# Turning the probabilities one step later, and four key sub-blocks moved between the layers

## The reference

```python
q_a = to_heads(rms_norm(c_q, q_gain) @ w_uq, MLA_HEADS)          # heads 0..3
o_a = causal_block_attention(q_a, k_a, kv_a[..., MLA_NOPE_DIM:])  # softmax(q k^T) v
o_b = causal_block_attention(q_b, k_b, v_b, cum_log_f)           # heads 4..9
o_c = dilated_mixture_attention(rope(q_c), rope(k_c), v_c)       # heads 10..15
x = layer_norm(DEEPNORM_ALPHA * x + mix @ w_out)
...
k, v = split(mem @ w_kv, 2)      # depends on mem and the layer's weights, not on x
x = layer_norm(DEEPNORM_ALPHA * x + softmax(q k^T / 16) v @ w_o)
gates = shared_group_router(x, router_w, router_bias)
x = layer_norm(DEEPNORM_ALPHA * x + moe_ffn(x, gates, w_gate, w_up, w_down))
```

## Time and profile before

| | |
|---|---|
| median of 3 runs | 820.36 us (818.98 to 822.27) |
| profiled execution: its own time | 822.08 us |
| profiled execution: span of the trace | 820.5 us |
| TensorE busy | 797.2 us, 97% of the span |
| VectorE busy | 634.1 us, 77% |
| ScalarE busy | 508.5 us, 62% |
| mean granted TensorE clock | 0.99 |

### The profile page before, as it was taken

One profiled execution on the slowest core, in us unless ns is written; L12 is line 12 of the kernel. 1 busy time (PEld: TensorE's weight loads), 2 busy tenths in 40 slices (PEclk: granted clock), 3 DMA queues, 4 the chain that ended last, 5 costly groups with the idle time before them and its releaser, 6 DMA issues.

```text
span 820.5 us, 12140 instructions
## 1 busy us (share of the span) xinstructions
PE 797.2 (97%) x4364; PEld 688.0 (84%) x4364; DVE 634.1 (77%) x1110; ACT 508.5 (62%) x804; POOL 78.4 (10%) x150
## 2 busy tenths in 40 slices
PE   7899999999999999999999999999999999999995
PEld 7899897789877888888899989877998788888884
DVE  5657868785658999999765586786846699999995
ACT  4755554554546788888555555554454567888873
POOL 3148200020000000000011350000200000000000
PEclk9999999999999999999999999999999999999998
DMA  8954443475334799999755644336643439999951
GB/s 289 344 182 155 144 135 130 139 228 157 105 126 134 246 368 367 364 370 374 259 150 146 209 142 154 105 129 204 209 129 99 145 120 342 367 369 364 370 209 52
DMA packets 122095, 177.06 MB, mean 216 GB/s; under 512 B 10177, under 2 KB 90577, under 8 KB 122033
## 3 DMA queue, kind: packets, MB, share of 16 engines
q1 hardware_dynamic: 120048, 169.56, 62.0%
q0 software_dynamic: 1984, 6.70, 2.9%
HBM read 175.18 MB, written 1.05 MB: 215 GB/s over the span
## 4 chain that ended last, share of the span: by engine, by line
PE 81%; DVE 10%; ACT 4%; issue 2%; DMA 2%; SPq 0%; POOL 0%; DVEq 0%; ACTq 0%; POOLq 0%
PE bank L1557 22%; PE bank L1559 22%; PE bank L1558 22%; DVE w_split L509 3%; DMA raw<-in_w_in_dram 2%; PE bank L1660 2%; PE bank L1724 2%; PE bank L1765 2%; PE bank L1870 2%; DVE xg_lo L1496 1%; ACT w_split L504 1%; PE bank L1756 1%; PE bank L1735 1%; PE bank L1713 1%; PE bank L1785 1%
## 5 line engine op out<-in xcount | busy, mean ns | idle before, releaser
L509 DVE TENSOR_TENSOR w_split<-raw,w_split 128x1024 fp32r<-128x1024 f32 (+3 forms) x336 | 386.0, 1173 | 69.8 <-ACT w_split L504 63.6
L504 ACT ACTIVATE w_split<-raw 128x1024 fp32r<-128x1024 f32 (+3 forms) x336 | 335.4, 1010 | 103.7 <-PE bank L1559 86.2
L1557 PE MATMUL bank<-w_split,xg_hi 128*128 128x512 f32 x256 | 102.9, 402 | 0.0
L1559 PE MATMUL bank<-w_split,xg_lo 128*128 128x512 f32 x256 | 100.1, 391 | 0.0
L1558 PE MATMUL bank<-w_split,xg_hi 128*128 128x512 f32 x256 | 99.9, 390 | 0.0
L1557 PE MATMUL bank<-w_split,xT_hi 128*128 128x384 f32 (+2 forms) x224 | 77.9, 348 | 3.1 <-DVE w_split L509 2.3
L1559 PE MATMUL bank<-w_split,xT_lo 128*128 128x384 f32 (+2 forms) x224 | 76.5, 341 | 0.0
L1558 PE MATMUL bank<-w_split,xT_hi 128*128 128x384 f32 (+2 forms) x224 | 76.2, 340 | 0.0
L1559 PEld LDWEIGHTS bank<-w_split,xg_lo 128*128 128x128 f32 x256 | 48.0, 188 | 10.3
L1557 PEld LDWEIGHTS bank<-w_split,xg_hi 128*128 128x128 f32 x256 | 48.1, 188 | 9.5 <-DVE xg_lo L1496 0.6
L1558 PEld LDWEIGHTS bank<-w_split,xg_hi 128*128 128x128 f32 x256 | 48.2, 188 | 9.0
(11 more groups left out here) (314 smaller groups left out, 1550.9 us busy)
## 6 DMA issues: line engine op xcount, KB each, us to landing
raw<-in_expert_w_gate_dram SPq DMA_DIRECT2D x128, 256.0 KB, 5.8
raw<-in_expert_w_up_dram SPq DMA_DIRECT2D x128, 256.0 KB, 7.8
raw<-in_expert_w_down_dram SPq DMA_DIRECT2D x64, 512.0 KB, 7.8
raw<-in_xattn_w_kv_dram SPq DMA_DIRECT2D x32, 512.0 KB, 4.1
raw<-in_w_in_dram SPq DMA_DIRECT2D x40, 384.0 KB, 4.0
raw<-in_w_mix_out_dram SPq DMA_DIRECT2D x16, 512.0 KB, 3.8
raw<-in_xattn_w_q_dram SPq DMA_DIRECT2D x16, 512.0 KB, 3.4
raw<-in_xattn_w_o_dram SPq DMA_DIRECT2D x16, 512.0 KB, 5.5
```

What stands on the lines that cost most here:

```text
L504: nc.scalar.activation(w_hi[:, i % SPL, 0:w], raw[:, i % RAW, 0:w], ACT.Copy).then_inc(hi_ready, 1)
L509: nc.vector.tensor_tensor(w_lo[:, i % SPL, 0:w], raw[:, i % RAW, 0:w], w_hi[:, i % SPL, 0:w].bitcast(F32), ALU.subtract).then_inc(lo_ready, 1)
L1557: nc.tensor.matmul(o, lhs[0], rhs[0], start=first, stop=False, skip_group_check=shared)
L1559: return nc.tensor.matmul(o, lhs[1], rhs[0], start=False, stop=last, skip_group_check=shared)
```

## The change

It has three parts. First, `TURNED` and `VALUED`: the probabilities are turned in step s for head s-3 in place of s-2, the values are made for head s-4 in place of s-3, and there are 20 steps. On VectorE the normalisation in step s is that of head s-2, and it and the copy of the turned head stand ahead of the maximum of head s-1. `p_sb` and `pT` become one tile with three buffers of probabilities and two of turned ones for the 16 heads. The exponentials of the dilated heads no longer give sums, which were not used. Second, in layer 1 the job MK1 is replaced by ME1 (the same weights, the same product): its four sub-blocks stand at the head of layer 1's stream, in the places where TensorE made the unread products, in pair 3; they are copied out before the head steps. Layer 0 keeps MK1, and layer 1's filler has 25 sub-blocks. A's parts 0 and 1 are then split after the transposes of x. UKV goes from pair 3 to pair 1. Third, in layer 1 the jobs from MV0 on exchange pairs 0 and 1. The lines that only pass `l` to `banks`, `evac_a` and `evac_v` are left out below.

```diff
+TURNED, VALUED = 3, 4
...
+        if l:
+            subs += [(l, "ME1", j) for j in range(4)]
         for name, js in (("A", range(4)), ("FV", range(4)), ("FK", range(4)), ("FQ", range(2)), ("UQ", range(1)),
                          ("UKV", range(1)), ("FQ", range(2, 4)), ("DQ", range(4)), ("DK", range(4)), ("DV", range(4)),
-                         ("MK0", range(4)), ("MK1", range(4)), ("MV0", range(4)), ("WO0", range(3)), ("WO1", range(1)), ("WO0", range(3, 4)), ("WO1", range(1, 4)),
+                         ("MK0", range(4)), ("MK1", range(0 if l else 4)), ("MV0", range(4)), ("WO0", range(3)), ("WO1", range(1)), ("WO0", range(3, 4)), ("WO1", range(1, 4)),
...
-        p_sb, _ = sb("p_sb", [P, 2, 4 * P])
-        pT, _ = sb("pT", [P, 2, 4 * P])
+        probs, _ = sb("probs", [P, 16 * P])
...
-                ("UQ", 2, 0, 2), ("UKV", 0, 4, 3), ("FQ", 2, 0, 0), ("DQ", 2, 0, 1), ("DK", 2, 0, 0), ("DV", 0, 2, 1),
+                ("UQ", 2, 0, 2), ("UKV", 0, 4, 1), ("ME1", 2, 0, 3), ("FQ", 2, 0, 0), ("DQ", 2, 0, 1), ("DK", 2, 0, 0), ("DV", 0, 2, 1),
...
+        def left_out(l):
+            return "MK1" if l else "ME1"
+
+        def pair_in(l, name, k):
+            return 1 - k if l and k < 2 and job[name] >= job["MV0"] else k
+
+        pair = [{name: pair_in(l, name, k) for name, _, _, k in jobs} for l in range(L)]
+
+        def held_by(l, name):
+            return next((m for m, _, _, _ in reversed(jobs[:job[name]]) if m != left_out(l) and pair[l][m] == pair[l][name]), None)
...
-        slots = [3, 2, 2] + [2, 1] * 4 + [1, 2] * 2 + [1] * 4
+        slots = [[3, 2, 2] + [2, 1] * 4 + [1, 2] + [1] * 7] + [[3, 2, 2, 2] + [1] * 16] * (L - 1)
...
+            assert len(turns[l]) == HEADS + VALUED
...
+        def probs_of(h):
+
+            if h < HEADS:
+                return probs[:, (h % 3) * 3 * P:(h % 3 + 1) * 3 * P]
+            return probs[:, (h % 2) * 4 * P:(h % 2 + 1) * 4 * P]
+
+        def turned_of(h):
+
+            if h < HEADS:
+                return probs[:, (9 + h % 2 * 3) * P:(12 + h % 2 * 3) * P]
+            return probs[:, (8 + h % 2 * 4) * P:(12 + h % 2 * 4) * P]
+
+        def free_turns(h):
+
+            return h - 2 if h < HEADS else max(h - 1, HEADS)
...
-                if h >= 2:
-                    act.wait_ge(pt_done.sem, pt_done.at(l, h - 1))
+                if h >= 3:
+                    act.wait_ge(pt_done.sem, pt_done.at(l, free_turns(h)))
...
-                        src, scale = p_sb[:, h % 2, sl], 1.0
+                        src, scale = probs_of(h)[:, sl], 1.0
...
-                    acc = sm1 if MLA_H + FOX_H <= h < HEADS else sm
-                    nc.scalar.activation(p_sb[:, h % 2, sl], src, ACT.Exp, bias=nmx[:, h, t:t + 1], scale=scale,
-                                         accum_out=acc[:, h, t:t + 1]).then_inc(e_ready.sem, 1)
+                    total = {} if MLA_H + FOX_H <= h < HEADS else {"accum_out": sm[:, h, t:t + 1]}
+                    nc.scalar.activation(probs_of(h)[:, sl], src, ACT.Exp, bias=nmx[:, h, t:t + 1], scale=scale, **total)\
+                        .then_inc(e_ready.sem, 1)
...
+            def keys(l, name, c0):
+                wait_job(l, name)
+                for u, b in enumerate(banks(l, name)):
+                    nc.scalar.activation(kTx[:, c0 + 2 * u:c0 + 2 * u + 2, :], b[:, :].rearrange("p (c t) -> p c t", c=2),
+                                         ACT.Copy).then_inc(job_a.sem, 1)
...
-                if l == 0:
-                    split_hi(act, first)
+                split_hi(act, first)
...
-                    split_hi(act, first + 1)
+                split_hi(act, first + 1)
...
+                if l:
+                    act.wait_ge(split_free, free_at(index[l, "UKV", 0]))
+                    keys(l, "ME1", 4)
...
-                for s in range(HEADS + 3):
+                for s in range(HEADS + VALUED):
...
-                    for nm, r in (("MK0", 0), ("MK1", 1)):
-                        if index[l, nm, 3] in turns[l][s]:
-                            wait_job(l, nm)
-                            for u, b in enumerate(banks(nm)):
-                                nc.scalar.activation(kTx[:, 4 * r + 2 * u:4 * r + 2 * u + 2, :],
-                                                     b[:, :].rearrange("p (c t) -> p c t", c=2), ACT.Copy)\
-                                    .then_inc(job_a.sem, 1)
+                    if index[l, "MK0", 3] in turns[l][s]:
+                        keys(l, "MK0", 0)
+                    if l == 0 and index[l, "MK1", 3] in turns[l][s]:
+                        keys(l, "MK1", 4)
...
-                    if s >= 3 and (s - 3) % 2 == 1:
-                        evac_o(l, s - 3)
+                    if s >= VALUED and (s - VALUED) % 2 == 1:
+                        evac_o(l, s - VALUED)
...
-                    for j in range(2):
-                        split_hi(act, index[l + 1, "A", j])
+                    for j in range(3):
+                        split_hi(act, index[l + 1, "ME1", j])
                 y_of(l, NG - 1)
+                if l + 1 < L:
+                    split_hi(act, index[l + 1, "ME1", 3])
...
-                    if h >= 2:
-                        dve.wait_ge(pt_done.sem, pt_done.at(l, h - 1))
+                    if h >= 3:
+                        dve.wait_ge(pt_done.sem, pt_done.at(l, free_turns(h)))
...
-                if l == 0:
-                    split_lo(dve, first + 1)
+                if l:
+                    split_lo(dve, first)
+                split_lo(dve, first + 1)
...
-                for s in range(HEADS + 3):
+                for s in range(HEADS + VALUED):
                     for i in ahead_of[l][s]:
                         split_lo(dve, i)
                     if index[l, "DV", 3] in turns[l][s]:
                         copy_job(l, "DV", lambda t: dv[:, t, :, :], lambda b: heads_of(b, DIL_H, HD))
                     if index[l, "MV0", 3] in turns[l][s]:
                         copy_job(l, "MV0", lambda t: vx[:, t, 0:512], lambda b: b[:, :])
+                    if 2 <= s < HEADS + 2:
+                        softmax_norm(l, s - 2)
+                    if TURNED <= s < HEADS + TURNED:
+                        evac_pT(l, s - TURNED)
                     for h in scored(s):
                         softmax_max(l, h)
-                    if in_pair(s - 1) and s % 2 == 0:
-                        softmax_norm(l, s - 1)
-                    if 2 <= s <= HEADS + 1:
-                        evac_pT(l, s - 2)
-                    if 1 <= s <= HEADS and not (in_pair(s - 1) and s % 2 == 0):
-                        softmax_norm(l, s - 1)
-                    if s >= 3 and (s - 3) % 2 == 1:
-                        if l == 0 and s == 4:
+                    if s >= VALUED and (s - VALUED) % 2 == 1:
+                        if l == 0 and s == VALUED + 1:
                             dve.wait_ge(const_pool, 57)
-                        evac_o(l, s - 3)
+                        evac_o(l, s - VALUED)
                 for i in range(index[l, "WO1", 1], index[l, "XQ0", 0]):
...
-                    for j in range(2):
-                        split_lo(dve, index[l + 1, "A", j])
+                    for j in range(3):
+                        split_lo(dve, index[l + 1, "ME1", j])
                 y_of(l, NG - 1)
+                if l + 1 < L:
+                    split_lo(dve, index[l + 1, "ME1", 3])
...
+                elif l:
+                    ready(l, "ME1")
...
-                    keep_busy(20)
+                    gemm(index[l, "ME1", 0])
+                    gemm(index[l, "ME1", 1])
                 if l == 0:
                     warm(12)
                     pe.wait_ge(x_in[0], 16)
                 turn_x(l, "XT0", 0, -1)
                 if l:
-                    keep_busy(5)
                     pe.wait_ge(end_half.sem, end_half.at(l - 1, 1))
                     for f in range(KC):
                         if f == KC // 2:
                             pe.wait_ge(x_ready.sem, x_ready.at(l, 0))
-                        ins = nc.tensor.transpose(banks("XT1")[f // 4][:, (f % 4) * P:(f % 4 + 1) * P],
+                        ins = nc.tensor.transpose(banks(l, "XT1")[f // 4][:, (f % 4) * P:(f % 4 + 1) * P],
                                                   xs[:, 1, f * P:(f + 1) * P], ident[:, :])
                         if f == KC // 2 - 1:
                             ins.then_inc(begin_turned, 1)
                     ins.then_inc(turned.sem, 1)
-                    keep_busy(11)
+                    gemm(index[l, "ME1", 2])
+                    gemm(index[l, "ME1", 3])
...
-                for s in range(HEADS + 3):
+                for s in range(HEADS + VALUED):
                     for i in turns[l][s]:
                         gemm(i)
-                    if s >= 3 and (s - 3) % 2 == 1:
-                        head_values(l, s - 3)
-                    if 2 <= s <= HEADS + 1:
-                        head_turn(l, s - 2)
```

(4 more changed lines are left out.)

127 lines of the change are left out of this document (62 added, 65 removed).

## The result

The change made the kernel slower. Its median is 835.13 us (831.91 to 839.95, 4 runs) against 821.32 us (818.98 to 825.62, 4 runs) for the kernel before, on the same chip: a ratio of 1.0167, with a 95% interval of 1.0099 to 1.0235. The forecast was 810.3, and faster. The profiled execution took 833.79 us for a span of 832.2 us, 11.7 above the span of before.

A forecast was written before the change was run, and what follows sets the result against it. The prediction took TensorE to bound the kernel, with VectorE second. Its terms, -11.5 + 4.0 - 2.6 = -10.1 us, took the median of 820.36 to 810.3 us, with ends of 807.8 and 813.1 and an 8-in-10 range of 806.5 to 815.0.

The forecast's parts named there:

- What bounds the kernel: Head steps: TensorE is the bound, busy 97% of the span, with VectorE second and close in the dilated part.
- Keys out of the head steps: Layer 1's head steps: 96 key matmuls at 0.12 us leave, taking 11.5 us off.
- Keys between the layers: Between the layers: key sub-blocks replace unread products, so A starts 4.0 us later, with +3.2 as lower bound.
- that rival: Between the layers: the clock falls to half for one or two 3 us stretches, 812 to 813.5 us; chance 0.06.
- Copying the keys out, and the bank pairs: ScalarE's two key copies go into an existing wait, and the moved or exchanged pairs cost nothing: 0 us.
- Turning a step later: Both layers' head steps: TensorE stalls of 2.0 us go, 0.7 returns through VectorE's work; 2.6 us gained together.
- Slower: All 40 head steps: maxima wait behind turned copies on VectorE, delaying TensorE's next scores; 825 us, chance 0.03.
- The change doesn't do what it says: Head steps: keys only covered latency, so steps last as before despite their removal; 821 us, chance 0.08.
- VectorE as the bound: Layer 1's dilated steps: VectorE takes the bound, costing some 3.5 us more in the last eight steps; 814 us, chance 0.13.
- The sum: Whole kernel: -11.5 + 4.0 - 2.6 = -10.1 us, from a median of 820.36 to 810.3 us.

The follow-up runs named there:

- e7: Changed kernel with ScalarE rounding the filler of the step after next ahead of the exponentials and finished values' copies moved ahead on both engines; 809.28 us.
- e14: As e7, but layer 1's keys are back in its filler and the unread products back between the layers; 817.91 us.
- e2: Changed kernel with only the later turning and its VectorE order: layer 1's keys back in its filler, unread products back between the layers; 836.96 us.
- e10: As e6, with the copies of the finished values also moved ahead on ScalarE and VectorE; 823.06 us.
- e12: Changed kernel with VectorE's order maximum, turned copy, values, normalisation, and on ScalarE early filler rounding and values first; 821.39 us.
- e1: Changed kernel with each step's maximum put ahead of the normalisation and the turned copy on VectorE; 824.83 us.
- e6: Changed kernel with the order edits of e1 (VectorE) and e4 (ScalarE) together; 828.84 us.
- e11: As e12, but the values' copies stay last on both engines; 832.62 us, a single time.
- e4: Changed kernel with ScalarE rounding the filler of the step after next ahead of the exponentials, VectorE's order unchanged; 822.09 us, one run.
- e9: Changed kernel with the old turning and VectorE order back, keys still between the layers, plus ScalarE's order of e4; 827.85 us.
- e8: Changed kernel with three unread one-column copies added on ScalarE behind the exponentials in steps 4 to 19; 843.22 us, a single time.

## Why the prediction was wrong, step by step

**What bounds the kernel.** TensorE did bound it before. But that VectorE and ScalarE had busy time to spare said nothing on their order, and I judged the new order by sums of work.

**Keys out of the head steps, -11.5.** Right as an amount: e7 and e14 differ by 100.2 - 88.7 = 11.5. In the changed kernel only 4.3 of it arrived (5.9 at full clock), since the ring and not TensorE's work set the length of most steps.

**Keys between the layers, +4.0.** Right: 4.2 in all, 3.9 from the first product to A. XT0 stood behind the second key block, where I had it: 5.8 us after the products' start by both. The wait on XT1 was 0.4. The clock stayed at 1.0, so that rival is out.

**Copying the keys out, and the bank pairs, 0.** No sign of a cost: e7, which has all of them, has no stall there.

**Turning a step later, -2.6.** This is the step of the prediction that failed. It says "It adds no instruction. What it can bring is the stalls of TensorE", and then "in the new order that wait goes, and what is late next is VectorE's own amount of work". The wait for the exponentials went, and its 2.0 us a layer with it: e14 gains 2.5 and 2.2. What was late next was not an amount: it was the maximum, behind the normalisation and the turned copy, and through it the exponentials, the rounding queued behind them on ScalarE, and the low part of the filler. Measured by e2, the term is +7.8 and +7.0, in place of -1.3 and -1.3. With both queues reordered (e14) it is -2.5 and -2.2. Before, the normalisation ran beside ScalarE's rounding and the copy of the turned head beside the exponentials, as the kernel before shows:

```profile
493.62 0.56 DVE L1097 COPY pT<-bank 128x384 f32<-128x384 f32 x1
493.74 0.40 ACT L746 ACTIVATE p_sb<-p_sb,nmx 128x128 f32<-128x128 f32 x1 [0.23 <-DVE nmx L1066]
...
494.89 1.05 ACT L504 ACTIVATE w_split<-raw 128x1024 fp32r<-128x1024 f32 x1
494.96 0.55 DVE L1089 TENSOR_SCALAR p_sb<-p_sb,ri 128x128 f32<-128x128 f32 x2
```

The change put both into the series.

**The rivals.** "Slower" had 0.03, and was nearly the mechanism: the turned copy ahead of the maximum on VectorE, in all steps, deciding at 0.37 us a step more than I counted. By e2 the head steps are 14.8 us longer than before where I had counted 2.6 less: 17.4 us over 40 steps, 0.44 a step. Where it went wrong is the link back to TensorE. I let the loop close through the scores, found 0.7 us of VectorE against a sub-block of 2.1 to 2.9, and called it safe. It closes through ScalarE's rounding, and is 4.89 us long against a step that TensorE does in 3.4 (489.86 less 486.45, the same step from maximum to maximum in e7). "The change doesn't do what it says" had the keys as cover: true of 7.2 of 11.5 us in the changed kernel (5.6 at full clock), and of 3.1 with the old turning. VectorE as the bound is refuted by e7, which gives VectorE the same work and needs 26.6 us less for the two layers' head steps than the changed kernel (100.3 + 88.7 against 110.5 + 105.2). The clock did fall, but in the head steps and not between the layers, see the last section.

**The sum.** In the changed kernel the terms came to -4.3 + 4.2 + 14.8 = +14.7, or 13.1 with the keys at full clock; the medians differ by 13.8. With the orders mended they are -11.5 + 4.2 - 4.7 = -12.0 us by the segments of e7 and e14, and e7's 809.28 us stands near the forecast of 810.3. That is no merit of the forecast: e7 has two orders that the change has not.

## What to carry to other kernels

In a kernel whose engines work fixed queues, a moved instruction is not costed by its own duration but by the ring that it lies in. Write down, for one step, who waits for whom across all queues, including the work that only stands behind a waiting instruction (here ScalarE's rounding of weights behind the exponentials), add up the distances, and compare with the step of the bounding engine, 4.89 against 3.4 us here. Put work that needs nothing from this step (the next filler's rounding) ahead of the instruction that waits, and let only true dependencies be in series. A change that loses may be one or two orders away from a gain: the parts of this one were worth 12 us once ScalarE rounded early and the finished values were copied first. The orders with the maximum first on VectorE, which looked as good on paper, came out level with the kernel before (e10, e12) or behind it (e1, e6, e11).

What stays open: why both orders together (e6) are slower than each alone, by 4.0 and some 6.8 us. Against the maximum first alone (e1) the loss is in layer 0, 109.2 against 106.4 us. The waits of both kinds are in it, but I did not follow the ring that results. Open too is what the values' place is worth without the early rounding, and with it how much of the changed kernel's loss is the rounding's alone.

## What the runs showed of the hardware that I had not expected

The granted clock can fall inside the head steps once TensorE has stalls there. It did so in seven of the changed kernels (the stars) and in none of the kernels without a stall, but e4, e9 and e10 had stalls there and no such stretch. Windows of the changed kernel in layer 0 and in layer 1 (columns as above, the clock third from the end):

```profile
76.00:78.00 2.00, 0.98 (x6) 1.01 (x7) 1.96 (x4) 1.85 (x4) 0.56 (x1) 1.00 0.02 5
78.00:80.00 2.00, 2.00 (x8) 2.00 (x7) 2.00 (x3) 0.00 (x0) 2.00 (x3) 0.55 0.80 269
...
534.00:536.00 2.00, 1.58 (x6) 1.36 (x7) 1.93 (x10) 1.42 (x2) 0.00 (x0) 0.90 0.25 72
536.00:539.00 3.00, 3.00 (x9) 1.89 (x10) 2.48 (x9) 0.00 (x0) 0.00 (x0) 0.50 0.54 175
```

After 0.98 us of work in 2, TensorE gets 0.55, and from 536 to 539, after 1.58 in 2, 0.50, the level of 1.2 GHz. It cost 1.6 us in layer 1 and nothing in layer 0 (the distances stand below the table of runs). The likely reason is that in layer 0 VectorE was busy 1.96 and 2.00 of 2 us and set the length of that step, so that TensorE had time to spare; this wasn't tested. In e8 the clock was at 0.57 from 503 to 507, and the ring's step shown above, in that stretch, was longer by the dose and no more. The Trainium skill (TensorE: Matmul & The Clock Gate, A second HAM failure mode: psum-queue depth-cycling) tells of a kernel in which short idle times between groups of matmuls make the clock fall and rise again; these rows agree in that half clock follows stretches with idle time in them. Behind the memory heads, at the router, where the code is the same in all runs, such stretches come and vary in length: from the first memory head's scores to the experts' first product it took about 68.2, 69.7 or 71.2 us, while the memory heads themselves took 29.7 each time. So a profiled execution can differ from its like by 1.6 or 3 us a layer without cause in the change.

Three tiny instructions on ScalarE took 0.28 us together from start to start, in e8, though the first of them to the last's end is 0.37: I had taken 0.2 for each. A duration overlaps the next start so much that a dose has to be measured before it is used.
